# Gate and up products of a mixture of experts with the weights stationary, and expert weights loaded as 8 KB runs

## The reference, cut to what matters

```python
D_MODEL = 1024; N_EXPERTS = 16; D_EXPERT = 256
h = jax.nn.silu(jnp.einsum('nd,edf->nef', xf, w_g)) * jnp.einsum('nd,edf->nef', xf, w_u)
out = jnp.einsum('nef,efd->nd', h * gates[..., None], w_d)
```

## Time and profile before

| | us |
|---|---|
| median of 3 runs | 571.22 |
| the runs | 571.22, 573.0, 571.02 |
| the profiled execution | 573.08 |
| span of the profiled execution | 571.1 |
| TensorE busy in it | 550.5 |
| VectorE busy | 212.7 |
| ScalarE busy | 167.1 |
| GpSimd busy | 98.1 |

### The profile page before, as it was taken

The page is one execution under the profiler, slowest core; times in us unless marked ns, Lnnn a source line. Parts: engine busy times, 40 slices in busy tenths (PEclk is TensorE's granted clock), DMA queues, the critical chain, the costliest instruction groups (busy, mean ns, idle before and its releaser), DMA issues.

```text
span 571.1 us, 6753 instructions
## 1 busy us (share of the span) xinstructions
PE 550.5 (96%) x2562; PEld 342.4 (60%) x2562; DVE 212.7 (37%) x528; ACT 167.1 (29%) x326; POOL 98.1 (17%) x116
## 2 busy tenths in 40 slices
PE   6999999999999999999999998999999999999984
PEld 5677755544454555565444445777767777776741
DVE  2443476523123332426333765622223223212138
ACT  6332596612112232222223254111212111211132
POOL 3016000115000000003100201423232323232100
PEclk8899999999999999999999999999999999999998
DMA  9999977899500000059510339899999999999574
GB/s 268 356 331 363 317 280 318 307 388 336 207 1 0 0 0 2 0 217 351 165 61 37 90 115 353 233 337 333 344 322 353 352 346 329 340 353 346 106 203 167
DMA packets 73636, 133.15 MB, mean 233 GB/s; under 512 B 4154, under 2 KB 49634, under 8 KB 71554
## 3 DMA queue, kind: packets, MB, share of 16 engines
q1 hardware_dynamic: 59008, 99.36, 50.4%
q0 software_dynamic: 9536, 28.75, 18.3%
q10 hardware_dynamic: 5058, 4.58, 2.4%
HBM read 117.47 MB, written 18.35 MB: 238 GB/s over the span
## 4 chain that ended last, share of the span: by engine, by line
PE 90%; DVE 5%; ACT 2%; issue 1%; DMA 1%; ACTq 0%
PE psum L725 85%; PE psum L728 6%; DVE arena L2214 1%; DMA hy<-in_c_sample_dram 1%; DVE x L2219 1%; ACT arena L1373 1%; ACT L1373 0%; DVE arena L2272 0%; DVE arena L2133 0%; ACT uT L1373 0%; ACTq L1613 0%; ACT hy L1373 0%; DVE uT L1795 0%; DVE arena L2317 0%; ACT ss L1373 0%
## 5 line engine op out<-in xcount | busy, mean ns | idle before, releaser
L725 PE MATMUL psum<-ring,arena 128*128 128x256 f32 (+1 forms) x640 | 171.7, 424 | 2.3 <-DVE arena L2272 1.8
L725 PEld LDWEIGHTS psum<-ring,arena 128*128 128x128 f32 x640 | 119.2, 190 | 39.5 <-issue 27.1
L725 PE MATMUL psum<-ring,uT 128*128 128x512 f32 (+1 forms) x384 | 126.5, 522 | 0.0
L1373 ACT ACTIVATE arena<-psum 128x512 f32<-128x512 f32 (+6 forms) x111 | 51.0, 480 | 226.0 <-PE psum L725 209.1
L725 PEld LDWEIGHTS psum<-ring,uT 128*128 128x128 f32 (+1 forms) x384 | 56.5, 172 | 60.1 <-issue 55.8
L725 PE MATMUL psum<-uT,ring 128*128 128x288 f32 x256 | 66.5, 417 | 1.3 <-ACT uT L1373 1.3
L725 PEld LDWEIGHTS psum<-uT,ring 128*128 128x128 f32 x256 | 48.8, 194 | 18.0 <-issue 5.1
L728 PEld LDWEIGHTS psum<-con,arena 128*128 128x128 f32 (+1 forms) x295 | 36.3, 147 | 19.9 <-issue 13.5
L728 PE MATMUL psum<-con,arena 128*128 128x128 f32 (+1 forms) x295 | 43.1, 284 | 3.3 <-DVE arena L1788 1.8
L1373 ACT ACT_TABLE_LOAD x33 | 42.3, 1283 | 3.1 <-issue 2.1
L2317 DVE TENSOR_TENSOR arena<-arena,psum 128x256 f32<-128x256 f32 x16 | 6.7, 422 | 93.2 <-ACT arena L1373 93.2
(11 more groups left out here) (214 smaller groups left out, 430.6 us busy)
## 6 DMA issues: line engine op xcount, KB each, us to landing
ring<-in_w_mod_dram SPq DMA_DIRECT2D x24, 1024.0 KB, 10.3
ring<-in_w_exp_gate_dram SPq DMA_DIRECT2D x16, 1024.0 KB, 9.7
ring<-in_w_exp_up_dram SPq DMA_DIRECT2D x16, 1024.0 KB, 16.3
ring<-in_w_exp_down_dram SPq DMA_DIRECT2D x16, 1024.0 KB, 10.4
ring<-in_w_in_dram SPq DMA_DIRECT2D x10, 1024.0 KB, 11.7
ring<-in_w_out_dram SPq DMA_DIRECT2D x4, 1024.0 KB, 21.4
f_dram<-in_consts_dram POOLq DMA_DIRECT2D x1, 3072.0 KB, 19.5
arena<-in_state_ret_dram POOLq DMA_DIRECT2D x6, 512.0 KB, 5.6
```

The lines of the kernel that those rows point to most:

```text
L725: return nc.tensor.matmul(out, lhsT, rhs, start=first, stop=last)
L1373: return nc.scalar.activation(out, src, func, **kw).then_inc(done, 1)
```

## The change

- The gate and up products exchange their operands. The weights are stationary, in blocks of 128 inputs by 128 hidden values, and the 128 token slots of `xgT` are streamed. The result is already the transposed hidden tile: gate in bank 0 (two blocks), up in banks 1 and 6. There are 32 products of 128 columns where there were 16 of 256.
- `turn_hidden`, its PSUM-to-SBUF copy on ScalarE and their two semaphores are gone. VectorE writes the hidden product straight to `hT`, as two instructions of 128x128, one for each block of hidden values.
- `expert_out(e)` stands after the token transposes and the slot counting of the same iteration, for all experts, and its loops are exchanged: hidden block outside, output half inside. It waits for each block of `hT` by itself.
- The results are taken and scattered one iteration earlier (`take_out(e)`, `add_rows(e - 3)`).
- SiLU starts when the gate blocks are done; `s_in` counts three per expert (gate, first up block, second up block). The gate slot of the ring is free after the gate blocks.
- Weight rows are laid out as `(p k)`: partition p holds 8 (for down 2) consecutive rows, one run of 8 KB. The operands follow: block k of the tokens takes every 8th column of `xg` (32 bytes apart), and hidden block m takes every second column of the gate and up weights (8 bytes apart).

The diff without the two semaphores' declaration and the lines that only change a count:

```diff
--- before.py
+++ after.py
@@ -433,7 +431,7 @@
             elif kind == "out":
                 used[p] = (s_out, TILES)
             elif kind in ("wg", "wu"):
-                used[p] = (s_in, a + 1)
+                used[p] = (s_in, 3 * a + (1 if kind == "wg" else 3))
             else:
                 used[p] = (s_down, a + 1)
         expert_pieces = [p for p in weight_pieces() if p[0] in ("wg", "wu", "wd")]
@@ -490,11 +488,11 @@
                         "(k p) n -> p k n", p=P)
                     dst = dst.rearrange("p (k n) -> p k n", n=512)
                 elif kind == "wd":
-                    src = w_exp_down[0, a].rearrange("(k p) n -> p k n", p=P)
+                    src = w_exp_down[0, a].rearrange("(p k) n -> p k n", p=P)
                     dst = dst.rearrange("p (k n) -> p k n", n=D)
                 else:
                     w = w_exp_gate if kind == "wg" else w_exp_up
-                    src = w[0, a].rearrange("(k p) n -> p k n", p=P)
+                    src = w[0, a].rearrange("(p k) n -> p k n", p=P)
                     dst = dst.rearrange("p (k n) -> p k n", n=FE)
                 sp.dma_start(dst, src).then_inc(landed[slot[p]], 16)
 
@@ -700,7 +698,7 @@
                         out_offset=bass.IndirectOffsetOnAxis(ap=add_tok[:, e:e + 1], axis=0))\
                         .then_inc(s_ost[e % 2], 16)
 
-                for e in range(NE + 3):
+                for e in range(NE + 2):
                     if 0 < e < NE:
                         gather_input(e)
                     if e == 1:
@@ -711,8 +709,8 @@
                             .then_inc(s_fready, 16)
                     if 2 <= e < NE + 1:
                         gather_gates(e - 2)
-                    if e >= 4:
-                        add_rows(e - 4)
+                    if e >= 3:
+                        add_rows(e - 3)
             pool.wait_ge(s_store, 16 * 5)
             pool.wait_ge(s_ssto, 16 * 2)
             for k in range(2):
@@ -1232,49 +1230,42 @@
                         pe.wait_ge(s_xgTd, e)
                     for k in range(KT):
                         last = turn(bank[2 + k // 4][:, (k % 4) * P:(k % 4 + 1) * P],
-                                    xg[e % 2][:, k * P:(k + 1) * P])
+                                    xg[e % 2].rearrange("p (i k) -> p k i", k=KT)[:, k, :])
                     last.then_inc(s_xgT, 1)
-
-                def expert_out(e):
-                    wd = weights(pe, ("wd", e, 0)).rearrange("p (k n) -> p k n", n=D)
-                    pe.wait_ge(s_hte, e + 1)
-                    if e >= 1:
-                        pe.wait_ge(s_eoa, e)
-                        pe.wait_ge(s_eod, e)
-                    for c in range(2):
-                        for k in range(FT):
-                            last = mm(bank[4 + c][:], hT[e % 2][:, k * P:(k + 1) * P],
-                                      wd[:, k, c * 512:(c + 1) * 512], k == 0, k == FT - 1)
-                        if c == 0 and e == NE - 1:
-                            last.then_inc(s_down, 1)
-                    last.then_inc(s_down, 1)
 
                 def expert_in(e):
                     wg = weights(pe, ("wg", e, 0)).rearrange("p (k n) -> p k n", n=FE)
                     wu = weights(pe, ("wu", e, 0)).rearrange("p (k n) -> p k n", n=FE)
                     pe.wait_ge(s_xgTa, e + 1)
                     pe.wait_ge(s_xgTd, e + 1)
-                    if e == 1:
-                        pe.wait_ge(s_snew, 2)
-                    if e >= 2:
-                        pe.wait_ge(s_hm, e - 1)
-                    for j, w in enumerate((wg, wu)):
-                        for k in range(KT):
-                            if e >= NE - 2 and j == 0 and k == KT // 2:
-                                expert_out(e - 1)
-                            last = mm(bank[e % 2][:, j * FE:(j + 1) * FE], xgT[e % 2][:, k, :],
-                                      w[:, k, :], k == 0, k == KT - 1)
-                    last.then_inc(s_in, 1)
-
-                def turn_hidden(e):
-                    pe.wait_ge(s_hm, e + 1)
-                    if e == 0:
-                        pe.wait_ge(s_snew, 2)
                     if e >= 1:
-                        pe.wait_ge(s_hte, e)
+                        pe.wait_ge(s_hs, e)
+                        pe.wait_ge(s_hm, FT * e)
+                    for w, outs in ((wg, (bank[0][:, 0:P], bank[0][:, P:FE])),
+                                    (wu, (bank[1][:, 0:P], bank[6][:, 0:P]))):
+                        if e == 0 and w is wu:
+                            pe.wait_ge(s_snew, 4)
+                        for m, out in enumerate(outs):
+                            for k in range(KT):
+                                last = mm(out, w.rearrange("p k (i m) -> p k m i", m=FT)[:, k, m, :],
+                                          xgT[e % 2][:, k, :],
+                                          k == 0, k == KT - 1)
+                            if w is wu or m == FT - 1:
+                                last.then_inc(s_in, 1)
+
+                def expert_out(e):
+                    wd = weights(pe, ("wd", e, 0)).rearrange("p (k n) -> p k n", n=D)
+                    if e >= 1:
+                        pe.wait_ge(s_eoa, e)
+                        pe.wait_ge(s_eod, e)
                     for k in range(FT):
-                        last = turn(bank[6][:, k * P:(k + 1) * P], hg[e % 2][:, k * P:(k + 1) * P])
-                    last.then_inc(s_ht, 1)
+                        pe.wait_ge(s_hm, FT * e + k + 1)
+                        for c in range(2):
+                            last = mm(bank[4 + c][:], hT[e % 2][:, k * P:(k + 1) * P],
+                                      wd[:, k, c * 512:(c + 1) * 512], k == 0, k == FT - 1)
+                            if e == NE - 1 and k == FT - 1 and c == 0:
+                                last.then_inc(s_down, 1)
+                    last.then_inc(s_down, 1)
 
                 def turn_last(part):
 
@@ -1326,10 +1317,7 @@
                     else:
                         if e < NE - 1:
                             turn_last(e + AHEAD - NE)
-                    if 0 < e < NE - 2:
-                        expert_out(e - 1)
-                    turn_hidden(e)
-                expert_out(NE - 1)
+                    expert_out(e)
                 for t in END_ORDER:
                     add_last(t)
                     if t == 2:
@@ -1723,21 +1711,13 @@
                 take_input(0)
                 store_rest()
                 for e in range(NE):
-                    if e >= NE - 2:
-                        take_out(e - 1)
-                    act.wait_ge(s_in, e + 1)
+                    act.wait_ge(s_in, 3 * e + 1)
                     if e >= 2:
-                        act.wait_ge(s_hm, e - 1)
-                    f(hb[e % 2], bank[e % 2][:, 0:FE], ACT.Silu, s_hs)
+                        act.wait_ge(s_hm, FT * (e - 1))
+                    f(hb[e % 2], bank[0][:, 0:FE], ACT.Silu, s_hs)
                     if e + 1 < NE:
                         take_input(e + 1)
-                    if 0 < e < NE - 2:
-                        take_out(e - 1)
-                    act.wait_ge(s_ht, e + 1)
-                    if e >= 2:
-                        act.wait_ge(s_down, e - 1)
-                    f(hT[e % 2], bank[6][:, 0:FE], ACT.Copy, s_hte)
-                take_out(NE - 1)
+                    take_out(e)
                 f(softp[:, 0, 0:1], eps[:, 0:1], ACT.Sqrt, s_act)
 
                 for i, t in enumerate(END_ORDER):
@@ -2049,9 +2029,8 @@
                 dve.wait_ge(s_skv, h + 1)
                 for n, b in enumerate(((4, 5), (1, 6))[h - 2]):
                     part = s0[h % 2][:, 4 * n:4 * n + 4, :].rearrange("p b e -> p (b e)")
-                    last = v.scalar_tensor_tensor(out=part, in0=part, scalar=GAMMA_STEP[h],
-                                                  in1=bank[b], op0=ALU.mult, op1=ALU.add)
-                last.then_inc(s_snew, 1)
+                    v.scalar_tensor_tensor(out=part, in0=part, scalar=GAMMA_STEP[h], in1=bank[b],
+                                           op0=ALU.mult, op1=ALU.add).then_inc(s_snew, 1)
 
             for t in range(TILES):
                 rotate(t, 0)
@@ -2307,21 +2286,20 @@
                 for h in range(2, NH):
                     new_state(h)
                 for e in range(NE):
-                    if e >= NE - 2:
-                        take_out(e - 1)
                     if e + AHEAD < NE:
                         hits(e + AHEAD)
+                    if e >= 2:
+                        dve.wait_ge(s_down, e - 1)
                     dve.wait_ge(s_hs, e + 1)
-                    if e >= 2:
-                        dve.wait_ge(s_ht, e - 1)
-                    v.tensor_tensor(out=hg[e % 2], in0=hb[e % 2], in1=bank[e % 2][:, FE:2 * FE],
-                                    op=ALU.mult).then_inc(s_hm, 1)
+                    for m, up in enumerate((bank[1], bank[6])):
```

(18 more changed lines are left out.)

## The result

The changed kernel takes 577.09 us (median; 576.55 to 579.73), beside 571.12 us for the kernel before (570.23 to 573.0). The ratio is 1.0118, with a 95% interval of 1.0087 to 1.0148: slower by 1.2%. The forecast was 567.4 us, faster by 0.7%.

A forecast was written before the change was run, and what follows sets the result against it. TensorE's own instruction stream and its gaps were taken as the bound. Terms -3.5 +3.4 -0.85 -0.91 -1.6 -0.3 gave -3.8 us, from the median of 571.22 to 567.4 us; range 565.0 to 581.5.

The forecast's parts named there:

- Hidden transposes: Experts' stage, TensorE: the two transposes of the hidden tile go, 0.22 us for each of 16 experts, -3.5 us.
- gaps after expert 0 (-0.85), before expert 15 (-0.91) and after it (-1.6): TensorE's stalls and slow starts at the first and last experts, closed by the new order of work.
- end: Last combination: VectorE's wait for rows of f_dram goes, as expert 14 is scattered earlier; gain 0.3 us.
- The form of the products: Gate and up products: 64 records at 111.25 ns, 7.12 us against 6.91 per expert, +3.4 us for 16.
- The 8 byte step: Stationary gate and up weights read with a step: taken at no cost, upper bound 109 us for 16 experts.
- Rival 2: The step in the stationary gate and up weights slows their loads: 10 ns each gives 577.6 us; chance 0.05.
- The 32 byte step: Gathered tokens read with a step in the 8 transposes: taken at no cost, upper bound 13.6 us for 16 experts.
- rival 1: The step in the tokens slows their loads in the 8 transposes per expert: 574.2 to 581.0 us; chance 0.28.
- The loads: Weight loads in 8 KB packets, slots freed slightly earlier: costed at nothing, since nothing waits for weights.
- The cover of the new waits: Transposes and slot counting, 1.0 us, hide the down product's wait for VectorE's hidden product; no cost in middle experts.
- rival 3: GpSimd's scatter chain becomes the bound, sharing DMA engines with larger packets: 7 us, 574.5 us; chance 0.07.
- Rival 4: The gain doesn't come: products at 113 ns or a new wait in a gap's place, 569 to 571 us; chance 0.10.

The follow-up runs named there:

- E3: The changed kernel with the rows of all expert weights laid out as before: no operand has a step, packets of 1 and 4 KB; 568.4 us, ratio 0.9948.
- E1: The changed kernel with each stationary weight block made of adjacent columns and the down weights' rows loaded to match; 568.35 us, ratio 0.9949.
- E5: The changed kernel with 16 instead of 8 bytes between the stationary gate and up columns (wrong columns multiplied); 694.55 us, ratio 1.2144.
- E6: The changed kernel with 32 instead of 8 bytes between the stationary gate and up columns (wrong columns multiplied); 698.9 us, ratio 1.2225.
- E9: The changed kernel with the token transposes written as ordinary products with the identity moving, 16 records per expert instead of 8; 624.62 us, ratio 1.0928.
- E4: The kernel before with only the new layout: 8 KB runs, stepped transposes, weights still moving, old order; 574.48 us, ratio 1.0048.
- E7: The changed kernel with only an eighth (gate, up) or half (down) of each weight piece loaded for experts 4 to 15; 577.32 us, ratio 1.0096.

## Why the prediction was wrong

- **Hidden transposes (-3.5), gaps after expert 0 (-0.85), before expert 15 (-0.91) and after it (-1.6), end (-0.3).** Right as a whole. E3 has these, and no step and no new wait at the ranks: 568.4 us against a forecast of 567.4. In the changed kernel's trace each gap is gone.
- **The form of the products (+3.4).** Right in kind, a little small: adjacent operands run at 111.7 ns, not 111.25 (7.15 us against 7.12 per expert, +0.5 in all).
- **The 8 byte step: this is the step that failed.** The prediction wrote "I take none for either, because the only rows there are say so". But rows of contiguous operands are not rows of stepped ones; they were only the lower bound. The truth was +6.1 ns a record, +6.2 us, more than the whole gain of 3.8. The same part had the argument for caution: about 106 of 111 ns is filling columns, so "whatever slows the load slows the stream". Rival 2 had the price nearly right ("even 10 ns per load costs 10.2 us"), with a chance of 0.05. At 1024 loads, 4 ns each would have undone the forecast, and that break-even was not worked out.
- **The 32 byte step (rival 1, 0.28).** False as a cause: no cost in pace (E1 against E3: 568.35 and 568.4). Its load did get slower, 141 to 188 ns. Its upper bound, the fill twice over (+106 ns), is a little less than what products pay: +120 ns at 16 bytes (E5), +125 at 32 (E6), and E9 shows it on the tokens themselves. The wrong assumption was that a transpose pays as a product does.
- **The loads, "at nothing, both ways": the second failure.** Only those who wait for the weights were asked about. The larger packets delay other queues: the stores of token rows, and with them the ranks, by 2.0 us. The search for cover should have been made at each DMA that something waits for while SP's loads are in flight. The earlier trace rows stood for the middle of the experts alone.
- **The cover of the new waits, and rival 3.** The cover held: the first half of the hidden product at 415.91, the second at 417.70, the down product at 418.50. Over the middle experts TensorE has no wait, so the scatters set nothing. Rival 4 (no gain, 113 ns) named the right kind of thing, with about a quarter of its size (1.75 ns a record).
- **The sum.** -3.8 forecast, +6.2 for the step, +0.5 for the pace without it, +2.0 at the ranks: +4.9. The traces differ by 5.2 like for like, the medians by 6.0. The rest is not placed. Part of it may be the lower clock after the wait at the ranks, which E4 to E7 show and the profiled execution of the changed kernel doesn't; whether its other executions had it is not recorded.
- **The range** of 565.0 to 581.5 held the time, but by way of a rival that is false: that is luck.

## What to carry to other kernels

Before weights are made stationary with a step, multiply the number of loads by a few nanoseconds and compare that with the gain: a stream of 128-column products is bound by its loads, and 1024 of them turn 6 ns into 6 us. Where it is free which columns make up a block, let a block be adjacent columns (E1, with the down rows loaded to match: 8.7 us less than the changed kernel, 6.2 of it from the step and 1.6 from the wait at the ranks). Put what needs a longer step (32 bytes here) into a transpose rather than a product. When a load's packets get larger, look not only at who waits for that load but at the small stores and gathers of other queues in flight beside it; in this kernel each of three times of issue for the same 4 MB hit another of them.

## What the runs showed of the hardware that I had not expected

- Stationary f32 columns of a product: 192 ns a load adjacent, 196 at 8 bytes, 329 at 16, 335 at 32; pace 111.7, 117.8, 231 and 237 ns a record. The edge lies between 8 and 16 bytes.
- A transpose with 32 bytes between columns: load 188 ns instead of 141, pace unchanged at 110 ns. The same operand in a product: 334 ns and 238 ns a record.
- Halving the DMA traffic (336 to 179 GB/s) changed nothing in TensorE's pace.
- Three stores on ScalarE's queue took 3.6 us to issue where the four 1 MB loads had landed before, 9.8 beside those loads in packets of 1 and 4 KB, 17.9 where all four had 8 KB, and 19.3 where two of the four had.
- After 4.6 us in which TensorE stood idle, its clock was granted at a mean of 0.69 over the next 13 us; the same group of 64 records took 10.12 instead of 7.78 us. After standing for 1.3 to 1.6 us at the ranks it was granted 0.72 to 0.76 over the next 6 to 7 us in some executions (E4 to E7), 1.6 us lost each time, and 1.00 in others.
